# Scan outputs as tokens by channels in a hybrid encoder layer, and a branch product whose first two slots run within the last scan steps

## What is computed

```python
def step(S, inp):
    r_t, w_t, k_t, v_t, kk_t, a_t = inp
    sa = -jnp.einsum('dbhij,dbhj->dbhi', S, kk_t)
    S = (S * w_t[..., None, :] + sa[..., :, None] * (kk_t * a_t)[..., None, :]
         + v_t[..., :, None] * k_t[..., None, :])
    return S, jnp.einsum('dbhij,dbhj->dbhi', S, r_t)
...
return out[0] + jnp.flip(out[1], axis=1)
...
mean = jnp.mean(o, axis=-1, keepdims=True)
var = jnp.mean(jnp.square(o - mean), axis=-1, keepdims=True)
o = ((o - mean) * lax.rsqrt(var + RWKV_GN_EPS)).reshape(B, T, RWKV_WIDTH)
o = o * gn_w + gn_b
return (o + bonus) * g
...
merged = sigmoid(gate_a) * (y_a @ w_branch_a[i]) + sigmoid(gate_b) * (y_b @ w_branch_b[i])
```

## Time and profile before

| | |
|---|---|
| median of three runs | 2369.81 us |
| profiled execution | 2367.51 us, its span from first to last instruction 2365.7 us |
| TensorE matmul busy | 2317.4 us (98%) |
| VectorE busy | 1510.5 us (64%) |
| ScalarE busy | 1104.3 us (47%) |
| mean granted TensorE clock | 0.997 |

### The profile page before, as it was taken

One profiled execution on the slowest core, in us unless ns is written; L12 is line 12 of the kernel. 1 busy time (PEld: TensorE's weight loads), 2 busy tenths in 40 slices (PEclk: granted clock), 3 DMA queues, 4 the chain that ended last, 5 costly groups with the idle time before them and its releaser, 6 DMA issues.

```text
span 2365.7 us, 32698 instructions
## 1 busy us (share of the span) xinstructions
PE 2317.4 (98%) x12307; PEld 1899.5 (80%) x12307; DVE 1510.5 (64%) x2003; ACT 1104.3 (47%) x1456; POOL 131.4 (6%) x209
## 2 busy tenths in 40 slices
PE   8999999999999999999999999999999999999998
PEld 6888888888887878778877777887888888888886
DVE  5666754666756666997963556666667664466665
ACT  5454443444445665555565323444544443444443
POOL 1000000000000002221011210000000000000000
PEclk9999999999999999999999999999999999999999
DMA  7666666666665756678677212765766666666654
GB/s 246 196 194 195 189 196 194 188 198 192 194 195 178 232 170 189 198 218 288 198 225 206 85 42 99 233 234 164 220 194 190 196 192 195 194 190 195 195 194 145
DMA packets 229697, 451.51 MB, mean 191 GB/s; under 512 B 23420, under 2 KB 25744, under 8 KB 228176
## 3 DMA queue, kind: packets, MB, share of 16 engines
q1 hardware_dynamic: 207872, 399.82, 55.1%
q0 software_dynamic: 11600, 45.31, 5.8%
q10 hardware_dynamic: 10112, 4.83, 0.8%
HBM read 427.35 MB, written 22.54 MB: 190 GB/s over the span
## 4 chain that ended last, share of the span: by engine, by line
PE 90%; DVE 4%; DMA 2%; ACT 2%; issue 1%; POOL 0%; ACTq 0%; DVEq 0%; SPq 0%; POOLq 0%
PE ps L1616 27%; PE ps L1618 27%; PE ps L1617 27%; DVE wlo L999 1%; DMA raw<-in_w_in 1%; PE ps L1976 1%; PE ps L2017 1%; PE ps L2002 1%; PE ps L2018 1%; PE ps L1977 1%; PE ps L1992 1%; DMA xin<-dif_dram 1%; PE ps L2033 1%; PE ps L2037 0%; DVE h L1088 0%
## 5 line engine op out<-in xcount | busy, mean ns | idle before, releaser
L999 DVE TENSOR_TENSOR wlo<-raw,whi 128x1024 fp32r<-128x1024 f32 (+1 forms) x760 | 929.8, 1228 | 691.2 <-ACT whi L516 686.4
L516 ACT ACTIVATE whi<-raw 128x1024 fp32r<-128x1024 f32 (+1 forms) x760 | 800.8, 1058 | 944.1 <-PE ps L1618 898.4
L1616 PE MATMUL ps<-whi,uhi 128*128 128x512 f32 (+1 forms) x2272 | 897.0, 395 | 8.2 <-DVE ulo L1038 4.1
L1618 PE MATMUL ps<-whi,ulo 128*128 128x512 f32 (+1 forms) x2272 | 885.8, 390 | 0.0
L1617 PE MATMUL ps<-wlo,uhi 128*128 128x512 f32 (+1 forms) x2272 | 885.4, 390 | 0.0
L1616 PEld LDWEIGHTS ps<-whi,uhi 128*128 128x128 f32 x2272 | 427.7, 188 | 106.2 <-issue 11.5
L1618 PEld LDWEIGHTS ps<-whi,ulo 128*128 128x128 f32 x2272 | 427.5, 188 | 89.0
L1617 PEld LDWEIGHTS ps<-wlo,uhi 128*128 128x128 f32 x2272 | 428.2, 188 | 84.6
L1616 PE MATMUL ps<-whi,hthi 128*128 128x512 f32 x704 | 274.0, 389 | 0.0
L1618 PE MATMUL ps<-whi,htlo 128*128 128x512 f32 x704 | 274.0, 389 | 0.0
L1617 PE MATMUL ps<-wlo,hthi 128*128 128x512 f32 x704 | 274.0, 389 | 0.0
(11 more groups left out here) (303 smaller groups left out, 1454.6 us busy)
## 6 DMA issues: line engine op xcount, KB each, us to landing
raw<-in_ffn_w_gu SPq DMA_DIRECT2D x352, 512.0 KB, 4.4
raw<-in_ffn_w_down SPq DMA_DIRECT2D x176, 512.0 KB, 4.4
raw<-in_w_in SPq DMA_DIRECT2D x160, 512.0 KB, 3.9
raw<-in_w_out SPq DMA_DIRECT2D x32, 512.0 KB, 4.0
raw<-in_w_branch_a SPq DMA_DIRECT2D x16, 512.0 KB, 4.2
raw<-in_w_branch_b SPq DMA_DIRECT2D x16, 512.0 KB, 3.9
gate_dram<-gst_g POOLq DMA_DIRECT2D x8, 512.0 KB, 5.4
gbuf<-gate_dram POOLq DMA_DIRECT2D x8, 512.0 KB, 4.8
```

The costliest lines, as they stand in the source:

```text
L516: nc.scalar.activation(whi[:, s, :, 0:p.width], raw[:, s, :, 0:p.width], ACT.Copy).then_inc(hi_ready, 1)
L999: V.tensor_tensor(wlo[:, s, :, 0:p.width], raw[:, s, :, 0:p.width], whi[:, s, :, 0:p.width].bitcast(F32), ALU.subtract).then_inc(lo_ready, 1)
L1616: mm(o, at, w_, start=(j == 0 and k == 0), stop=False)
L1618: return mm(o, bt, w_, start=False, stop=(j == p.slots - 1 and k == SB - 1))
```

## The change

- The outputs are products with tokens on the rows and the channels of a head on the columns (`half` in `recur`); both heads' outputs go to partitions 0 to 63 of bank 7, the next state to partitions 64 to 127 of the same bank. The diagonal blocks change place with the others in `sv`, `wt`, `ik` and the masks. In the backward direction the diagonal's operand and masks are read reversed (`scan_columns`), so that outputs come in the order of the tokens.
- ScalarE copies outputs to `oc` (forward) or a new tile `ob` (backward), in two operations; `to_oc` goes. `values` becomes two operations and moves behind the first state copy.
- Group norm works along the free dimension: sum, reduce, scale and subtraction (`gn_center`), reduce (`gn_variance`), a root and a reciprocal of four values a partition, a multiply (`gn_scale`), then two transposes on TensorE (`gn_turn`) and two operations on VectorE (`ya_out`). The products with `headsum` go.
- Values are turned by two transposes of 128x128 in place of four products (`values_t`), and in step 0 they stand before the W products.
- Alpha-beta goes to banks 2 and 3, values to 0, W to 1. `ends` is made one step earlier.
- `p_ya` takes its slots in the order of `YA_ORDER`; slots 0 and 1 are done in eight blocks of three products in steps 14 and 15, one behind each chunk's recurrence (`units`). `merge_a` moves accordingly.

```diff
-    p_ya, p_yb = (Pass(4, 4, 2, CW, lambda i, u, j, w=w: rows_cols(w[0], 0, j, (2 * i + u) * CW, CW), pairs)
-                  for w, pairs in ((w_branch_a, 2), (w_branch_b, 2)))
+    YA_ORDER = [(u, j) for u in range(2) for j in range(3)] + [(u, 3) for u in range(2)]
+    p_ya, p_yb = (Pass(4, 4, 2, CW, lambda i, u, j, w=w: rows_cols(w[0], 0, j, (2 * i + u) * CW, CW), order=order)
+                  for w, order in ((w_branch_a, YA_ORDER), (w_branch_b, None)))
...
-                nc.scalar.activation(sv[C:P, m % 2, :, :], ps[C:P, 2, :].rearrange("p (c v) -> p c v", c=NC_),
-                                     ACT.Copy).then_inc(vt_ready, 1)
+                for e in range(2):
+                    last = nc.scalar.activation(sv[0:C, m % 2, e::2, :],
+                                                ps[C * e:C * (e + 1), 0, 0:2 * P].rearrange("p (k v) -> p k v", v=P), ACT.Copy)
+                last.then_inc(vt_ready, 1)
...
+            def outputs(m):
+
+                b, d = m // 2, m % 2
+                act.wait_ge(o_mm, m + 1)
+                if d and b >= 2:
+                    act.wait_ge(gn_cent, b - 1)
+                chunks = ps[0:C, 7, :].rearrange("p (c v) -> p c v", c=NC_)
+                dst = (ob[:, b % 2, :] if d else oc[:, b, :]).rearrange("p (k v) -> p k v", v=P)
+                for e in range(2):
+                    last = nc.scalar.activation(dst[C * e:C * (e + 1), :, :],
+                                                chunks[:, ::-1, :][:, e::2, :] if d else chunks[:, e::2, :], ACT.Copy)
+                last.then_inc(o_ready, 1)
...
                     minus_w(m + 1)
-                    values(m + 1)
                 for c in range(NC_ - 1):
                     act.wait_ge(s_mm, 3 * m + c + 1)
-                    nc.scalar.activation(sv[0:C, m % 2, c + 1, :], ps[0:C, 2, 0:2 * C], ACT.Copy).then_inc(s_ready, 1)
+                    nc.scalar.activation(sv[C:P, m % 2, c + 1, :], ps[C:P, 7, c * P:(c + 1) * P], ACT.Copy).then_inc(s_ready, 1)
+                    if c == 0 and m + 1 < NM:
+                        values(m + 1)
+                    if c == 1 and m % 2 == 0 and m:
+                        gn_square(m // 2 - 1)
+                outputs(m)
                 if m < RING:
                     ahead(p_ya, [m])
-                b = m // 2 - 1
-                if m % 2:
-                    if b >= 0:
-                        gn_deviation(b)
-                else:
-                    if b >= 1:
-                        ya_high(b - 1)
-                    if b >= 0:
-                        gn_square(b)
+                if m % 2 == 0 and m:
+                    gn_deviation(m // 2 - 1)
+                if m % 2 and m >= 3:
+                    ya_high((m - 3) // 2)
...
             def gn_center(b):
-                dve.wait_ge(gn_mean, b + 1)
-                V.scalar_tensor_tensor(out=oc[:, b, :], in0=ps[:, 6, 0:T], scalar=-1.0 / C, in1=oc[:, b, :],
-                                       op0=ALU.mult, op1=ALU.add).then_inc(gn_cent, 1)
+
+                dve.wait_ge(o_ready, 2 * b + 2)
+                y = oc[:, b, :]
+                link(V.tensor_tensor(y, y, ob[:, b % 2, :], ALU.add))
+                link(V.tensor_reduce(GN_MEAN, by_head(y), AX.X, ALU.add))
+                link(V.tensor_scalar(GN_MEAN, GN_MEAN, 1.0 / C, None, ALU.mult))
+                V.tensor_tensor(by_head(y), by_head(y), GN_MEAN.unsqueeze(2).broadcast_to((P, 4, C)),
+                                ALU.subtract).then_inc(gn_cent, 1)
+
+            def gn_variance(b):
+                dve.wait_ge(gn_sq, b + 1)
+                V.tensor_reduce(GN_VAR, by_head(osq[:, b % 2, :]), AX.X, ALU.add).then_inc(gn_ms, 1)
 
             def gn_scale(b):
                 dve.wait_ge(gn_sqrt, b + 1)
+                y = by_head(oc[:, b, :])
+                link(V.reciprocal(GN_DEV, GN_DEV))
+                V.tensor_tensor(y, y, GN_DEV.unsqueeze(2).broadcast_to((P, 4, C)), ALU.mult).then_inc(gn_scaled, 1)
+
...
+            def ya_out(b):
+                dve.wait_ge(gn_t, b + 1)
                 dve.wait_ge(gn_in[b % 4], 32 * (b // 4 + 1))
                 y = oc[:, b, :]
-                link(V.reciprocal(rs[:, b % 2, :], rs[:, b % 2, :]))
-                link(V.scalar_tensor_tensor(out=y, in0=y, scalar=vec[:, R_GNW + b:R_GNW + b + 1],
-                                            in1=rs[:, b % 2, :], op0=ALU.mult, op1=ALU.mult))
-                link(V.scalar_tensor_tensor(out=y, in0=y, scalar=vec[:, R_GNB + b:R_GNB + b + 1], in1=bo[:, b % 4, :],
-                                            op0=ALU.add, op1=ALU.add))
-                V.tensor_tensor(y, y, gg[:, b % 4, :], ALU.mult).then_inc(ya_y, 1)
+                link(V.scalar_tensor_tensor(out=y, in0=ps[:, 6, 0:T], scalar=vec[:, R_GNW + b:R_GNW + b + 1],
+                                            in1=bo[:, b % 4, :], op0=ALU.mult, op1=ALU.add))
+                V.scalar_tensor_tensor(out=y, in0=y, scalar=vec[:, R_GNB + b:R_GNB + b + 1], in1=gg[:, b % 4, :],
+                                       op0=ALU.add, op1=ALU.mult).then_inc(ya_y, 1)
 
...
-                b = m // 2 - 1
                 if m % 2 == 0:
-                    if b >= 1:
-                        gn_scale(b - 1)
-                    if b >= 0:
-                        gn_center(b)
+                    if m:
+                        gn_variance(m // 2 - 1)
+                    if m >= 4:
+                        ya_low(m // 2 - 2)
+                elif m >= 3:
+                    ya_out((m - 3) // 2)
+
+            def norm_behind(m):
+
+                if m % 2:
+                    gn_center(m // 2)
+                elif m:
+                    gn_scale(m // 2 - 1)
+
+            dve.wait_ge(yb_ready, 4)
+            link(V.tensor_copy(m1r[:, C:4 * C], kc[:, K_M1 + C:K_MG]))
+            link(V.tensor_copy(m1r[:, 0:C], kc[:, K_M1:K_M1 + C][:, ::-1]))
 
             def masked_ab(m):
...
-                                    ps[:, h, :].rearrange("p (c v) -> p c v", c=2),
-                                    kc[:, K_M1:K_MG].unsqueeze(1).broadcast_to((P, 2, 4 * C)), ALU.mult).then_inc(ab_ready, 1)
+                                    ps[:, 2 + h, :].rearrange("p (c v) -> p c v", c=2),
+                                    (m1r[:, :] if m % 2 else kc[:, K_M1:K_MG]).unsqueeze(1).broadcast_to((P, 2, 4 * C)),
+                                    ALU.mult).then_inc(ab_ready, 1)
...
-                                    kc[:, K_MG:K_RESET].unsqueeze(1).broadcast_to((P, 4, 2 * C)), ALU.mult).then_inc(gh_ready, 1)
-
-            def to_oc(m):
-                b = m // 2
-                dve.wait_ge(o_mm, m + 1)
-                src = ps[:, 7, 0:T]
-                if m % 2:
-                    V.tensor_tensor(oc[:, b, :], oc[:, b, :], src[:, ::-1], ALU.add).then_inc(o_ready, 1)
-                else:
-                    V.tensor_copy(oc[:, b, :], src).then_inc(o_ready, 1)
+                    mask = by_head(kc[:, K_MG:K_RESET])[:, :, scan_columns(m)]
+                    V.tensor_tensor(gh[:, m % 2, 4 * h:4 * h + 4, :].rearrange("p c (w t) -> p c w t", w=2),
+                                    ps[:, 4 + h, :].rearrange("p (c w t) -> p c w t", c=4, w=2),
+                                    mask.unsqueeze(1).broadcast_to((P, 4, 2, C)), ALU.mult).then_inc(gh_ready, 1)
 
             for m in range(2):
                 masked_ab(m)
             masked_gh(0)
+            ends(2)
             dve.wait_ge(st_out[0], 16 * 7)
             dve.wait_ge(st_out[1], 16 * 7)
             for m in range(NM):
                 if m + 2 < NM:
-                    ends(m + 2)
                     masked_ab(m + 2)
                 else:
                     norm_between(m)
-                if m % 2 and m >= 5:
-                    ya_low(m // 2 - 2)
-                to_oc(m)
-                dve.wait_ge(o_ready, m + 1)
                 if m + 1 < NM:
                     masked_gh(m + 1)
+                if m + 3 < NM:
+                    ends(m + 3)
+                norm_behind(m)
                 if m < RING:
                     ahead(p_ya, [m])
 
-            gn_center(NPAIR - 1)
-            gn_scale(NPAIR - 2)
             ya_low(NPAIR - 2)
+            gn_variance(NPAIR - 1)
+            gn_scale(NPAIR - 1)
...
-            gn_scale(NPAIR - 1)
+            fill(RING + 2)
+            ya_out(NPAIR - 1)
             ya_low(NPAIR - 1)
             fill(4)
             merge_a(0)
-            for i in range(2):
-                fill(1)
-                yb_low(i)
+            fill(1)
+            yb_low(0)
+            merge_a(1)
+            fill(1)
+            yb_low(1)
+            fill(6)
+            merge_a(2)
             fill(2)
-            merge_a(1)
-            fill(4)
-            merge_a(2)
...
-                    o = ps[r, c // 2, (c % 2) * 4 * C:(c % 2 + 1) * 4 * C]
-                    mm(o[:, 0:2 * C], beta[r, m, c * C:(c + 1) * C], q[r, at:dd + 1:dd - at, :], start=True, stop=True)
```

(60 more changed lines are left out.)

88 lines of the change are left out of this document (44 added, 44 removed).

## The result

| | kernel before | changed kernel |
|---|---|---|
| median | 2368.98 us (2365.45 to 2372.09) | 2349.8 us (2346.81 to 2352.81) |
| ratio | 1 | 0.9922 (95%: 0.991 to 0.9935) |
| profiled execution, its span | 2367.51, 2365.7 | 2351.84, 2350.0 |

The change is faster, by 18.5 us by the ratio; my forecast was a gain of 14.1 and 2355.7.

A forecast was written before the change was run, and what follows sets the result against it. TensorE's timeline bounds the kernel. Gains of 14.1 us (steps), 2.8 (scan end) and -0.3 (entry), less 2.5 for the clock, make 14.1 off the median 2369.8: 2355.7, range 2351.5 to 2364.0.

The forecast's parts named there:

- the term of 1.51: Each scan step, W products to start of the state recurrence (T): 1.51 us, set by VectorE's two g/h masks.
- The entry, with its price for the clock: Start of the scan: TensorE idles 3.8 us for step 0's values; clock fall (chance 0.6) priced at 2.5 us.
- the tail: End of the scan, step 14 to the second branch product: 20.0 us becomes 17.2, gain 2.8.
- The wait of 0.87: Every second step, before the W products, behind a reciprocal of 1.75 us; goes when that takes 0.17.
- Turn: Odd steps from the third on: two norm transposes take 0.31 us, after a new wait of 0.51 for scaled outputs.
- Recurrence blocks: Each scan step: column halves run side by side, three blocks fall from 0.49 to 0.385 us, the last rises to 0.37.
- Rival 2: Scan steps: column halves do not run side by side, blocks of 0.54; gain 6.4 us, 2363.4; chance 0.17.
- Copies, reversed operand: Scan steps: ScalarE output copies take 0.38 us each without delaying the recurrence; the reversed moving operand in odd steps costs 0.
- rival 3: Entry of the scan: no fall of the clock; gain 16.6 us, 2353.2; chance 0.26.
- rivals 1 to 3: As forecast, 2355.7 (0.45); column halves not side by side, 2363.4 (0.17); no clock fall at the entry, 2353.2 (0.26).
- rival 5: Odd steps: norm chain late by over 0.5 us, or ScalarE's copies delay the recurrence; gain 4 to 7 or nothing; 0.07.
- rival 4: Whole scan: the clock falls again and again, each up to 3.4 us; slower, 2436 at half clock throughout; chance 0.05.

The follow-up runs named there:

- the run with one column half: Changed kernel, steps 2 to 13 with output products of chunks 1 and 2 written to the state's column half: 2353.16 us, one execution, beside 2362.7 for the kernel before.
- the run with half a mask: Changed kernel, from step 2 on the second g/h mask over half of its 512 columns: 2350.5 us, one execution, beside 2362.7 for the kernel before.
- the second comparison: Changed kernel, unedited, measured once more against the kernel before on the same chip: 2350.12 us, ratio 0.9928.
- the run with few value products: Kernel before, only one of the four value products in each step from the second on: 2366.12 us, ratio 0.9991.
- the version with both edits: Changed kernel, VectorE scaling the norm before column ends in even steps, GpSimd loading pair 0's values before the last gate store: 2345.4 us, ratio 0.9906.

## Why the prediction was right, and where it was not

The kernel became faster in the stages that I had named, in the main by the mechanisms that I had named, and by more than I had said. The step of the prediction that failed is the term of 1.51 from the W products to the recurrence, "the masks, not the value products", which I left as it was in each of the 14 steps: it measured 1.39, 1.7 us in all. The entry, with its price for the clock (1.0), and the tail (0.4) come after it. The rest of the miss, 2.8 us, is in no term of the sum.

**Bound and direction.** Right: TensorE's timeline is what became shorter, and all later work moved forward whole (870.26 and 870.22).

**Reciprocal and norm.** The wait of 0.87 went. The new operations took what I had put on them: reduce 0.42 (0.41 put), reciprocal 0.17, multiply 0.42. No alpha-beta mask waits for them.

**Turn.** Forecast 0.51 of wait and 0.31 for the turn; 0.45 (0.37 in the row) and 0.36 measured, so that the two errors nearly cancel (0.82 and 0.81), which is luck. The scaled outputs come 2.22 after W (1386.85 to 1389.07), not 2.41 (the terms that I gave for it add up to 2.43): I had placed the ends after the masks' 1.35, and they start at 1.20.

**Recurrence blocks.** 0.39 and 0.37 as forecast from the starts in the earlier trace rows, and the run with one column half shows that it is the halves. The Trainium skill (TensorE: Matmul & The Clock Gate, Part 3) has matmuls start and end in program order. Rival 2 rested on that, and the measurement decides against it here: blocks of 0.39, not 0.54.

**Value products: the step that failed.** I said that the masks set T and that the value products were worth nothing. They held T back by about 0.1 in every step but those behind the wait of 0.87, and stretched the first block behind it by 0.15 (0.64 before, 0.49 with few value products). Taking three quarters of them away in the kernel before gave 1.44 over the 14 steps; the forecast of the steps was short by 1.7. After the change TensorE's queue sets T, 1.39 after W, in all steps; 0.12 less than the 1.51 of my sum, 14 times, is 1.7. I took a gap of 0.16 between the masks' end and T for a hand-over, and did not look at what TensorE had in its queue in it.

**Entry.** The wait for the values came as forecast (3.8, measured 3.87), and so did the fall of the clock. Its price was mis-sized: 2.5 forecast, 1.2 to 1.6 measured, because the low stretch was 3.4 us long and not 6.7. With the low stretch of 6.8 us in the run with half a mask it was 2.0 to 2.4, close to my figure: I had the price of a long fall, and took its length for fixed.

**Tail.** Total right (2.8 and 3.2), by luck, since its make-up was not: the blocks of product are worth 1.06, and the rest comes from a shorter step 14, from the norm products and the wait that are no longer there, and from 0.7 in the branch product.

**Copies, reversed operand.** Two output copies take 0.76, as put (2x0.38), and in the steady steps TensorE waits for no ScalarE copy. Steps in both directions take 7.38, so the reversed operand is free.

**The range.** The terms add up: 1.7 + 1.0 + 0.4 is 3.1, which is 17.2 less 14.1, and with 17.2 the time would be 2352.6, inside the range. The other 2.8 us, down to 2349.8, are not in the parts that the change touches. Of these, 0.8 is the kernel before itself: I counted from 2369.8, and its median beside the result is 2368.98. The cause of the last 2.0 stays open; by the second comparison (a gain of 17.1) there is nothing left to explain, which speaks for scatter. Both measured ratios (0.9922 and 0.9928) hold a gain of 17.2 within their intervals, and the part ahead of the change ended anywhere from 1300.3 to 1308.6. The range took in the unknown prices, but not this scatter of a median of a few executions. That T and the fall were both on the cheap side at once was left out of it too. By its number alone the result is nearest to rival 3 (no fall of the clock, 2353.2), and the trace shows that the clock did fall. The chance of 0.88 for faster is the sum of rivals 1 to 3; with half of rival 5, as I wrote, it is 0.92.

**Repeated falls of the clock (rival 4).** None: 1.00 over the window of eight steps above, with waits of 0.37 and transposes in it. The Trainium skill (same page, Part 4) does not count transposes as activity. With two to four of them among some 110 matmuls a step, these runs do not test that.

## What to carry over

Two engines that finish within 0.2 us of each other can both set the start of what follows, as here: before an edit on one is costed at nothing, ask what the other still has in its queue, and whether its tail runs into the next block. Work put into waits is worth less than the waits: here half. Removing a wait at the head of a stage can expose a load behind it that was hidden; moving that load one place up its queue gave more (4.6 us) than any other single edit tried on the changed kernel.

## Of the hardware

- What a block of products costs depends on how they divide over the two column halves: eight 64-column passes take 0.39 us spread over both, and 0.61 in one.
- At the entry the clock fell behind one idle stretch of 3.87 us, and also behind 0.88 and 1.81 us with 16 W products between them. It did not fall in the kernel before, with 1.40, 0.88 and 0.34 at the same place. In the tail it fell in the run with few value products, 1.7 us behind the end of a wait of 1.33, and did not in the kernel before, which has the same wait there. So the waits alone do not tell whether it falls.
- Low stretches had different lengths at the same place: 3.4 and 6.8 at the entry (above), and 3.4, 6.8 or 10.2 ahead of the change. The one ahead of the change lasted from 1254.7 to 1264.9 in the version with both edits, and from 1253.9 to 1257.3 in that with one column half. A window inside the first:

```profile
1255.00:1264.50 9.50, 9.25 (x86) 7.16 (x87) 5.58 (x12) 3.41 (x5) 0.78 (x1) 0.50 1.03 276
```

That is a part of the scatter ahead of the change. Over all the traces, the time from the end of the idle stretch there to the last gate product is 46.7 to 46.9 us with a low stretch of 3.4, 48.3 to 48.4 with 6.8, and 49.2 to 49.7 with 10.2: up to 3 us. The larger part arises earlier: the idle stretch itself ends anywhere from 1253.5 to 1259.4. Why it sets off a longer or a shorter low stretch stays open.
